# Two-layer latent and context backbone on one core: the latents' first norm moved into the context's output projection, logits and projections in another order, a ring of five rows and three fixed weight slots

## What is computed

```python
for i in range(DEPTH):
    with_ctx = i < DEPTH - 1
    ...
    h  = rmsnorm(x_lat, norm1_g[i]) * (1.0 + sc1) + sh1
    hc = rmsnorm(x_ctx, norm1_g[i]) * (1.0 + csc1) + csh1
    y, yc = token_mixer(h, hc, w_in[i], ...)   # pool, gated linear attention, latent attention, gates
    x_lat = x_lat + g1 * y
    h2 = rmsnorm(x_lat, norm2_g[i]) * (1.0 + sc2) + sh2
    x_lat = x_lat + g2 * peer(h2, ...)
    if with_ctx:
        x_ctx = x_ctx + cg1 * yc
        ...
        x_ctx = x_ctx + cg2 * peer(hc2, ...)
return rmsnorm(x_lat, final_norm_g)
```

## Time and profile before

| what | value |
|---|---|
| three runs | 3698.64, 3703.15, 3708.10 us; median 3703.15 us |
| the profiled execution | 3708.92 us, its span 3706.9 us |
| mean granted clock of TensorE | 0.883 |
| busy: TensorE, VectorE, ScalarE, POOL | 2910.7, 1754.2, 1100.6, 837.4 us |
| moved by DMA | 1071.8 MB, of it 805.4 MB by gathers, mean 289 GB/s |
| chain of work that ended last | TensorE 57%, DMA 24%, VectorE 8%, ScalarE 7% |

### The profile page before, as it was taken

One profiled execution on the slowest core, in us unless ns is written; L12 is line 12 of the kernel. 1 busy time (PEld: TensorE's weight loads), 2 busy tenths in 40 slices (PEclk: granted clock), 3 DMA queues, 4 the chain that ended last, 5 costly groups with the idle time before them and its releaser, 6 DMA issues.

```text
span 3706.9 us, 42712 instructions
## 1 busy us (share of the span) xinstructions
PE 2910.7 (79%) x16338; PEld 1824.3 (49%) x16338; DVE 1754.2 (47%) x4348; ACT 1100.6 (30%) x3076; POOL 837.4 (23%) x772
## 2 busy tenths in 40 slices
PE   7889998879889999687865655588899885555655
PEld 4777887555556766254521111167788761111111
DVE  1323012447575546645666776513311146766674
ACT  3122101243554443324432232231320122233332
POOL 0000000113223232322244444300000013444442
PEclk8999999889999999788887777789999997777777
DMA  7653442577888999987799999931224269999996
GB/s 297 240 200 148 152 155 102 231 293 288 319 305 350 382 393 381 364 345 289 280 389 410 415 420 414 384 137 49 100 103 149 90 242 405 411 414 414 420 415 272
DMA packets 151107, 1071.77 MB, mean 289 GB/s; under 512 B 16564, under 2 KB 18228, under 8 KB 22520
## 3 DMA queue, kind: packets, MB, share of 16 engines
q0 software_dynamic: 110592, 805.36, 54.0%
q1 hardware_dynamic: 40312, 263.69, 19.0%
HBM read 1067.93 MB, written 1.05 MB: 288 GB/s over the span
## 4 chain that ended last, share of the span: by engine, by line
PE 57%; DMA 24%; DVE 8%; ACT 7%; issue 3%; POOL 1%; DVEq 0%; ACTq 0%; SPq 0%; POOLq 0%
PE bank L364 43%; DMA ring<-in_experts,eid 21%; PE bank L378 11%; DVE ring L1284 4%; DMA weights<-in_quads 3%; POOL ring L1690 1%; PE bank L457 1%; ACT topk_work L854 1%; ACT topk_work L847 1%; PE bank L391 1%; ACT hT L907 1%; ACT topk_work L844 1%; ACT scratch L895 0%; ACT L942 0%; PE bank L577 0%
## 5 line engine op out<-in xcount | busy, mean ns | idle before, releaser
L1690 POOL DMA_INDIRECT ring<-in_experts,eid x768 | 837.2, 1090 | 2832.0 <-PE bank L378 1512.4
L378 PE MATMUL bank<-ring,topk_work 64*64 64x512 f32 x6144 | 984.3, 769 | 571.8 <-ACT topk_work L854 565.3
L1284 DVE CUSTOM_DVE_ANT_0 ring<-ring,h2tok 128x1024 f32<-128x1024 f32 x768 | 936.7, 1224 | 540.0 <-DMA ring<-in_experts,eid 535.0
L378 PEld LDWEIGHTS bank<-ring,topk_work 64*64 64x64 f32 x6144 | 236.3, 159 | 1235.7 <-ACT topk_work L854 921.9
L364 PE MATMUL bank<-hT,weights 128*128 128x256 f32 (+1 forms) x1968 | 461.9, 394 | 49.7 <-DMA weights<-in_quads 27.5
L364 PEld LDWEIGHTS bank<-hT,weights 128*128 128x128 f32 (+1 forms) x1968 | 371.2, 191 | 154.9 <-issue 42.1
L844 ACT ACTIVATE topk_work<-topk_work 128x2 f32<-128x2 f32 x384 | 77.9, 203 | 1156.6 <-DVE topk_work L1284 1143.3
L854 ACT ACTIVATE topk_work<-const,topk_work 128x64 f32<-128x64 f32 x768 | 226.2, 341 | 1.7 <-PE bank L378 0.8
L364 PE MATMUL bank<-hT,ring 128*128 128x256 f32 (+1 forms) x864 | 198.5, 390 | 5.2 <-ACT hT L907 4.6
L847 ACT ACTIVATE topk_work<-topk_work 128x1 f32<-128x1 f32 x768 | 184.6, 287 | 12.6
L1182 DVE COPY ab<-bank 128x256 f32<-128x256 f32 (+1 forms) x116 | 42.8, 369 | 297.1 <-PE bank L364 297.1
(11 more groups left out here) (205 smaller groups left out, 2991.6 us busy)
## 6 DMA issues: line engine op xcount, KB each, us to landing
weights<-in_quads SPq DMA_DIRECT2D x137, 1024.0 KB
ring<-in_quads SPq DMA_DIRECT2D x98, 1024.0 KB, 4.8
ring<-in_experts,eid POOLq DMA_INDIRECT x768
weights<-in_quads SPq DMA_DIRECT2D x7, 768.0 KB
ring<-in_quads SPq DMA_DIRECT2D x5, 768.0 KB, 6.0
weights<-in_quads SPq DMA_DIRECT2D x12, 256.0 KB
xT<-in_xT SPq DMA_DIRECT2D x1, 2048.0 KB, 11.0
out<-hT SPq DMA_DIRECT2D x1, 1024.0 KB, 4.5
```

The lines of the kernel that those rows point to most:

```text
L378: x = nc.tensor.matmul(acc[g][out, :], diag[mine, J % 4, :], ring[mine, J % RING, D + h * 512:D + (h + 1) * 512], start=first, stop=J % TI ...
L1284: v.tensor_tensor_reduce(row, row, h2tok[:, u // UNITS % 2, :], 1.0, 0.0, ALU.mult, ALU.add, dots[:, u % 2, j:j + 1]).then_inc(S["dot_done ...
L1690: pool.indirect_dma_start(ring[:, J % RING, :], None, d["experts"], bass.IndirectOffsetOnAxis(eid[:, u % 2, j:j + 1], 0)).then_inc(gathere ...
```

## The change

- `RING` goes from 6 to 5, `FIXED` from 2 to 3, `EXTRA` from 4 to 2: five slots in place of six without rows, three in place of two beside them. The ring and the fixed slots together keep their 8 MB.
- The plan's constants change: `PER_LOAD` 2.6 to 2.5, `LAG` 6 to 5, `LEAD_CHOICE` 14 to 10, 0.1 more for each job, 0.2 for each pair; VectorE's `deep` is always 2.
- `HT` and `GT` become two buffers `H[0]` and `H[1]` that swap their parts in pass 1. With that, the norm1 of pass 1 is done during `wo` of pass 0: TensorE sums after its second quad, VectorE inverts and scales before it evicts `y` 4, ScalarE squares and shifts after the last gate.
- In a full pass the logits `z` come after `q`, in pass 2 after the first two quads of `v`.
- The squares of the linear attention's output come in the middle of `r`, one root for both halves; `glat` comes after `vv`, and `vv` before `kn`. VectorE waits for the last `glat` before it writes `kn`.

```diff
-RING = 6
+RING = 5
 BANKS = 6
-FIXED, EXTRA = 2, 4
-PER_LOAD, LANDS, LAG = 2.6, 2.0, 6.0
-LEAD_CHOICE = 14.0
+FIXED, EXTRA = 3, 2
+PER_LOAD, LANDS, LAG = 2.5, 2.0, 5.0
+LEAD_CHOICE = 10.0
 DIAG_LAG = 3.0
...
-        HT = sb("hT", [P, DC, TS])
-        GT = sb("glaT", [P, DC, TS])
+        H = [sb("h_even", [P, DC, TS]), sb("h_odd", [P, DC, TS])]
...
+        def h_of(n):
+            return H[n == 1]
+        def gla_of(n):
+            return H[n != 1]
...
             def full(ins, *key):
                 ins.then_inc(*mark("psum_full", ("full",) + key))
                 full_now[key] = plan.now
+                plan.now += 0.1
...
-                plan.now = max(plan.now, landing + LAG)
+                plan.now = max(plan.now, landing + LAG) + 0.2
                 row_pair(n)
...
                 if p.full:
                     for q in range(2):
                         w = quad(i, "q", q, k=DC)
-                        project(n, "q", w, pair_of(q), HT, DC)
+                        project(n, "q", w, pair_of(q), h_of(n), DC)
                         beside(n, "q%d" % q)
+                    gate_logits(p)
                 for q in range(4):
                     w = quad(i, "v", q, k=DC)
-                    project_tokens(n, "v", q, w, HT, DC)
+                    project_tokens(n, "v", q, w, h_of(n), DC)
                     beside(n, "v%d" % q)
+                    if q == 1 and not p.full:
+                        gate_logits(p)
...
                 if p.full:
-                    for t in range(2):
-                        pe.wait_ge(*at("gla_fin", n, t))
-                        for g in range(2):
-                            b = job("glat", n, t, g)
-                            ...
                     for name in ("qn", "qr"):
                         ...
+                w = quad(i, "vv", k=2)
+                pe.wait_ge(*at("kvn_", n, 1))
+                for q in range(4):
+                    project_tokens(n, "vv", q, w[:, :, q * TS:(q + 1) * TS], kvd, 2)
+                if p.full:
+                    for t in range(2):
+                        pe.wait_ge(*at("gla_fin", n, t))
+                        for g in range(2):
+                            b = job("glat", n, t, g, loose=True)
+                            ...
                 w = quad(i, "kn", k=2)
...
                 for q in range(4):
                     w = quad(i, "wo", q, k=DC)
                     project(n, "y", w, pair_of(q), B, DC)
+                    if n == 0 and q == 1:
+                        square_sums("norm1", 1, DC, loose=True)
...
-                square_sums("norm1", n, DC)
+                if n != 1:
+                    square_sums("norm1", n, DC)
...
                             root("kvn", n, KVR, scr[:, 2, 0:TS])
+                            for tt in range(2):
+                                act.wait_ge(*at("o_sum", n, tt))
+                                for h in range(GLA_H):
+                                    x = nc.scalar.activation(scr[:, tt, 0:DV], ...
+                                                             ACT.Square, accum_out=small[:, 24 + 4 * tt + h:25 + 4 * tt + h])
+                                    ...
+                            nc.scalar.activation(small[:, 32:40], small[:, 24:32], ACT.Sqrt, bias=eps, scale=1.0 / DV).then_inc(
+                                *mark("act_step", ("gsqrt", n)))
...
+                if n == 0:
+                    squares("norm1", 1, DC, XT, span(1))
+                    root("norm1", 1, D, rstd1[:, :])
+                    shift("norm1", PASSES[1], SH1)
...
-                    deep = 2 if n % TILE_PAIRS == 3 else 3
+                    deep = 2
...
                 for c in range(DC):
+                    if n == 0 and c == 4:
+                        inverse("norm1", 1, rstd1[:, :])
+                        scale_rows("norm1", 0, PASSES[1], rstd1[:, :])
                     b = bank_of("y", n, c)
...
-                if n == 1 or n == 2:
-                    dve.wait_ge(*at("full", "ht", n - 1, 1, 1))
```

More of the change, by code:

```diff
@@ L627, in mixer @@
                     breathe()
+            def mixer(p):
+                n, i, s = p.n, p.i, p.s
+                for k in range(DC):
+                    pe.wait_ge(*at("h", "norm1", n, k))
+                w = quad(i, "lr", k=DC)
+                project(n, "lr", w, [(0, 0, RANK), (1, RANK, RANK)], h_of(n), DC)
+                beside(n, "lr")
+                for q in range(2):
+                    w = quad(i, "k", q, k=DC)
+                    project(n, "k", w, pair_of(q), h_of(n), DC)
+                    beside(n, "k%d" % q)
                 if p.full:
@@ L956, in mixer @@
                     beside(n, "v%d" % q)
+                    if q == 1 and not p.full:
+                        soft_gates(p)
                 units = gla_units(s)
@@ L1060, in mixer @@
                     beside(n, "qr")
+                for q in range(4):
+                    b = bank_of("vv", n, q, 1)
+                    if s and q == 0:
+                        act.wait_ge(*at("evicted", "s", n, 3, 1, 1))
+                    copy_out((VVltok if s else VVctok)[:, 1, q * TS:(q + 1) * TS], b[:, 0:TS], "vv", n, q, 1)
+                if p.full:
+                    for t in range(2):
+                        for g in range(2):
+                            b = bank_of("glat", n, t, g)
+                            if t == 0 and g == 0:
+                                act.wait_ge(*at("gla_fin", n, 1))
+                            bv = b[:, :].rearrange("p (c t) -> p c t", c=4)
+                            for m in range(2):
+                                x = nc.scalar.activation(gla_of(n)[:, g * 4 + m:g * 4 + m + 3:2, tokl(t)], bv[:, m:m + 3:2, :],
+                                                         ACT.Copy, scale=V(V_GLA + m, 1, i))
+                            x.then_inc(*mark(ACT_EV, ("evicted", "glat", n, t, g)))
                 for h in range(MLA_H):
@@ L1065, in mixer @@
                 beside(n, "kn")
-                for q in range(4):
-                    b = bank_of("vv", n, q, 1)
-                    copy_out((VVltok if s else VVctok)[:, 1, q * TS:(q + 1) * TS], b[:, 0:TS], "vv", n, q, 1)
             def latent_attention(n, s):
@@ L1392, in mixer @@
                     beside(n, "q1")
+                    log_gates(p)
                 for q in range(4):
@@ L1543, in mixer @@
                     norm_kv()
-                for h in range(0, MLA_H, 2):
-                    b = bank_of("kn", n, h)
-                    copy_out((KNl if s else KNc)[:, h, :], b[:, 0:TS], "kn", n, h)
-                beside(n, "kn")
                 for q in range(4):
@@ L1550, in mixer @@
                     copy_out((VVltok if s else VVctok)[:, 0, q * TS:(q + 1) * TS], b[:, 0:TS], "vv", n, q, 0)
+                for h in range(0, MLA_H, 2):
+                    b = bank_of("kn", n, h)
+                    if h == 0 and p.full:
+                        dve.wait_ge(*at("full", "glat", n, 1, 1))
+                    copy_out((KNl if s else KNc)[:, h, :], b[:, 0:TS], "kn", n, h)
+                beside(n, "kn")
             def latent_attention(n, s):
```

140 lines of the change are left out of this document (59 added, 81 removed).

## The result

| | before | after |
|---|---|---|
| median of the runs beside each other | 3701.35 us (3698.64 to 3708.1, 4 runs) | 3844.03 us (3833.61 to 3861.65, 4 runs) |
| ratio, 95% interval | 1 | 1.0388 (1.0346 to 1.0429) |
| span of the profiled execution | 3706.9 us | 3831.6 us |

The change costs 143 us. The forecast was 3678 us with a range from 3640 to 3733: the direction was wrong, and the time lies outside the range.

What follows compares the result with a forecast made beforehand. TensorE bounds passes 0 and 3, TensorE and DMA nearly both pass 1, the DMA the row-only stretches. Terms +20 - 7 - 19 - 15 - 9 + 5 = -25 us from the 3703.15 us median gave 3678 us, range 3640 to 3733.

Steps and rivals of the forecast that it cites:

- A turn needs 5.40 + 3.68 = 9.08 us at full clock and 5.40 + 4.58 = 9.98 us at the half: Row loop with five slots: gather latency plus processing for four rows, against the DMA's 9.92 us; cost +20 us.
- the prediction's rows: The 468 rows with nothing beside them, each predicted to lose 0.05 us at most with five slots.
- The rival that the ring starves: Rows with nothing beside them: latency 6.4 us, +75 us in place of +20, whole 3733 us; chance 0.20.
- The signs I had named: Signs of error: last-stretch rows 2.65 us apart or more, DMA share under 0.95; time over 3735 us.
- Norm1: Pass 1's start: sums moved into pass 0's output projection remove TensorE's wait for the shifted input; -7 us.
- `glat`: Full passes: earlier squares and later `glat` remove TensorE's waits for the gated output, 6.5 us a pass; -19 us.
- the discount: Pass 1: TensorE time freed there partly comes back as waits for rows not yet landed; +5 us.
- Third fixed slot: The three `queries`: one more quad loaded ahead halves TensorE's 29.7 us of weight waits; -15 us, ends 0 and -30.
- Logits after `q`: Pass 3: `v` still hides the 19 us to the last gate; 0 us, with pass 1 ends -10 and +5.
- The plan: Pass 1, 1140 to 1470: 3 more pairs beside TensorE's work, 3.05 us each; -9 us, ends -30 and +15.
- Rows take what TensorE gains: Pass 1 and its `queries`: rows set the end, so TensorE's gains there bring nothing; 3700 us; chance 0.15.
- More rows beside the passes: 1700 to 1895: third slot and denser plan move ten pairs there, -30 us more, 3648 us; chance 0.15.

Runs made afterwards that it cites:

- experiment 5: Changed kernel with six ring slots, two fixed and four extra slots and the old `deep`, keeping the new plan constants: 3636.34 us, ratio 0.9811.
- experiment 1: Kernel before, with its last group's gathers held back to five, then four rows in flight: 3883.95 us.
- experiment 3: Kernel before with only the ring at five, three fixed slots and two extra ones: 3958.54 us, ratio 1.0705.
- experiment 4: Changed kernel, five slots kept, with ScalarE taking the two rows of a pair one by one: 3616.69 us, ratio 0.9774.
- experiment 2: Changed kernel with six ring slots, two fixed slots, old plan constants and depth; moved norm1, `glat` and logits stay: 3656.09 us, ratio 0.9895.
- experiment 7: Changed kernel, five rows, with two fixed slots in place of three and three extra ones: 3903.89 us, ratio 1.055.
- experiment 11: Changed kernel with six rows, two fixed slots, old plan, and pass 1's norm1 put back at its start: 3681.09 us, ratio 0.9941.
- experiment 12: Changed kernel with single rows, six ring slots, two fixed slots, the old `deep` and the new plan constants: 3626.74 us, ratio 0.9791.
- experiment 8: Kernel before, with two, three, four and six gathers in flight in its last group: 4191.81 us.
- experiment 9: Kernel before, with only ScalarE taking the two rows of a pair one by one: 3684.38 us, ratio 0.9947.

## Why the prediction was wrong

**The step that failed** is "A turn needs 5.40 + 3.68 = 9.08 us at full clock and 5.40 + 4.58 = 9.98 us at the half". The number of rows in a turn (four) was right and so was the processing (4.40 us in the mean). The latency was not: 5.40 us belongs to a gather that finds the DMA idle, and in a loop that keeps four or five in flight it is 7.78. The turn is 12.18 us against the 9.92 that the DMA needs, so 0.485 us a row are lost by the pace measured (3.04 - 2.555): an estimate of 468 x 0.485 = 227 us over the prediction's rows in place of +20, and of 212 over the 437 that the changed kernel has in the two stretches (192 and 245). Experiment 5 against the changed kernel measures 214, ring, third slot and `deep` together. Experiment 1 shows the pace in code that has nothing else of the change, experiment 3 with nothing but the slots beside it, and experiment 4 takes the loss away with the five slots kept. That the two 227, this estimate and the gain of experiment 4, are the same number is chance. The rows that would have told it stood in the same trace, in the burst that the earlier trace rows begins: its second gather takes 6.65 us to its dot product, its third, issued at 3053.70, has it at 3061.52, 7.8 us later, and its fourth takes 9.15.

The Trainium skill ("DMA: Bandwidth & Descriptors", section on the anatomy of one SWDGE DMA) gives, as an estimate from its formula, 4.4 us for such a transfer, which I had set aside for the trace's 5.40. A lone gather measures 5.4 to 5.5 here, and neither number is the latency in the loop.

**The rival that the ring starves** had the place and the mechanism, and its condition ("from a latency of 5.7 us on") was met. Its price was not: I gave it 6.4 us and +75, on the notion of a late issue. The measured 7.78 us makes the 227 above. Nor was an issue late: the mean issue is 1064 ns after and 1090 before. The Trainium skill's rule on POOL and VectorE ("SBUF - State Buffer", section on the two separate sides), which I had put beside this rival, is not borne out as its cause: of every eight pairs, VectorE also chooses experts during the first four; there the mean latency of second rows is 7.70 to 8.42 us by place, 7.93 together, in the other four 7.34 to 7.90, 7.63 together. (Second rows alone. Whether these operations of VectorE run on both ports no run here shows, and VectorE's work could not be taken out, so an effect of the size of the 0.3 us is not excluded; the miss was 2.4.)

**The signs I had named.** Rows 2.65 us apart or more: 3.03, right. "A DMA share under 0.95": 0.94 and 0.95, at the border, and useless; the bytes had fallen by 15%. "One over 3735 that five slots cost more than a late issue": this is what came.

**The other terms** had the right sign, and most were too small:
- Norm1: -7. The wait went. Measured -17 with 12 to either side, 9.6 of it seen in the trace. TensorE of the changed kernel, around those sums:

```profile
559.73 6.85 PE L372 MATMUL bank<-ab,weights 128*128 128x256 f32 x31
566.42 4.64 PE L372 MATMUL bank<-scratch,const 128*128 128x256 f32 x16
570.89 13.98 PE L372 MATMUL bank<-ab,ring 128*128 128x256 f32 x64
```

- `glat`: -19 for three passes, 6.5 us each. The waits are gone, and each was worth more, because TensorE came out of it at the half clock. TensorE before, in pass 3, and windows around that wait (columns as in the earlier trace rows):

```profile
2613.46 0.59 PE L364 MATMUL bank<-krope,const 128*128 128x256 f32 x2
2620.08 1.97 PE L677 MATMUL bank<-const,dr 128*128 128x128 f32 x8 [6.02 <-DVE dr L1532]
2622.57 1.97 PE L677 MATMUL bank<-const,dr 128*128 128x128 f32 x8 [0.52 <-DVE dr L1532]
```

```profile
2612.00:2620.00 8.00, 2.05 (x10) 1.47 (x8) 1.83 (x5) 6.04 (x19) 0.00 (x0) 0.78 0.37 131
2620.00:2624.00 4.00, 3.40 (x15) 3.01 (x16) 1.87 (x6) 1.96 (x7) 0.00 (x0) 0.50 0.01 4
2624.00:2630.00 6.00, 6.00 (x24) 5.14 (x23) 0.00 (x0) 2.77 (x8) 0.00 (x0) 0.77 0.00 0
2630.00:2640.00 10.00, 10.00 (x48) 8.79 (x48) 0.88 (x3) 1.92 (x5) 0.00 (x0) 1.00 0.58 206
```

  The clock is 0.50 of full, 1.2 GHz, after the wait, and 2.4 GHz again in the window from 2630. In experiment 2, with the transposes after `vv`, they take 1.75 us in one piece:

```profile
2594.22 1.91 PE L701 MATMUL bank<-const,dr 128*128 128x128 f32 x16
2595.97 7.07 PE L371 MATMUL bank<-gla_work,ring 128*128 128x256 f32 x32
```

  Before, wait and transposes took from 2614.05 to 2624.33, 10.3 us: 8.5 us a pass, about -26 in place of -19, by the trace of this one pass. It was not undone alone.
- The three moves together: -7 - 19 + 5 (the discount) = -21 against the measured 39, with 11 to either side. The discount had no ground: pass 2 starts 45 us earlier in experiment 2, so what TensorE gains in pass 1 is not taken by rows. (The job of 3.45 us, on which these terms draw, is 3.50 by the earlier trace rows, 13.98 / 4; no term turns on it.)
- Third fixed slot: -15, with ends 0 and -30. At five slots -60 (experiment 7), beyond my end.
- Logits after `q`: 0. Not tried alone. It is inside the 39 us of the three moves and not told apart there.
- The plan: -9, ends -30 and +15. -31 at six slots, with 14 to either side, -58 at five with single rows, on or beyond my far end. The step that the prediction priced, 3.05 us a pair, holds; the number of pairs moved was 12 in place of 3, since I read the gain off one stretch (1140 to 1470) and the plan works in all of pass 1.

In ratios the way from the kernel before over experiments 2 and 5 to the changed kernel is -39 (moves) - 31 (plan) + 214 (ring, third slot and `deep`) = +144. That it meets the 143 follows from how it is put together and proves nothing; the parts are not independent. With the old constants and order, ring and slots cost 261 us (experiment 3).

**The other rivals.** "Rows take what TensorE gains" (0.15) did not happen (experiment 11, and the 61 us up to pass 2). "More rows beside the passes" (0.15) did in part: with the ring left at six the changed kernel takes 3636 us, and 3648 was the rival's time, with 12 pairs moved where it had ten. But its place was wrong. They pass beside pass 1 (experiment 5), not in 1700 to 1895, where the share was 0.76 and is 0.78 in the changed kernel, so that the nearness of the two times is partly luck. Its chance was joined to a ring that could not carry it.

## What to carry to other kernels

In a loop of transfers over few buffers, write the turn as latency plus processing over the number of transfers in a turn, and take the latency from a transfer issued while others move, never from the first one into an idle queue; it rises further as the queue fills (7.78 us here with two rows of the loop outstanding, 8.6 with three), so check the turn with the latency of the state that you aim at. Where the turn comes near the DMA's own time, the buffer count is the number to touch last: here one slot cost about 0.5 us a row. When a buffer must go, release buffers at a finer grain first: here that one edit was worth 227 us at five slots and 7 to 20 at six (7 with the new plan, experiment 12 against 5, which is within the noise). Judge a DMA-bound stretch by bytes a second, not by its share of busy time.

## What the runs showed of the hardware that I had not expected

- The latency of a gather of 128 rows of 8 KB grows with company: 5.5 us alone, 7.5 behind one other (experiment 8), 7.8 to 8.8 with five in flight (the changed kernel), 8.5 to 9.5 with six (the kernel before), where the DMA is full. Throughput follows the number in flight: 6.9, 5.2, 3.5, 3.0, 2.54 us a row for two, three, four, five, six.
- The DMA's share of busy time fell only from 1.00 to 0.94 while its bytes fell from 411 to 345 GB/s. At four in flight it was 0.82 with 299 GB/s (experiment 1), at two 0.42 with 149 (experiment 8, 3090 to 3400).
- A wait of 6 to 7 us costs TensorE 2 to 2.5 us more than itself, by the half clock that follows: experiment 11 (7.03 us, then 16 matmuls in 6.03 us in place of 3.5, at 0.50 of full in 693 to 696) and the transposes before (6.02 us, then 3.94 us in place of 1.91).
- With rows released singly TensorE's clock in the row stretches is lower: 0.69 in experiment 9 (3000 to 3600) against 0.75 before, both with six slots, and yet the rows come 2.51 us apart in place of 2.55. There the lower clock costs nothing, since the DMA sets the pace.
